# Four reorderings in a fused two-block transformer kernel on one core: first decay-scaled keys on ScalarE, VN additions ahead of the turns' low parts, gating scalings one step later, second norm block turned sooner

## The reference

```python
# block 1, delta rule: one step of the scan over chunks (both directions; the kernel uses chunks of 128)
v_new = u_i - einsum('bhcd,bhde->bhce', w_i, state)
o     = einsum('bhcd,bhde->bhce', q_i * exp(g_i), state) + einsum('bhcs,bhse->bhce', a_i, v_new)
k_dec = k_i * exp(g_last - g_i)
state = state * exp(g_last) + einsum('bhcd,bhce->bhde', k_dec, v_new)
# block 2
att = forgetting_attention(q, k, v, log_f)             # softmax((q k)/8 + c_i - c_j), causal
vg  = rmsnorm(vg, v_gain)                              # per group of 64: vg / sqrt(mean(vg^2)+eps) * gain
sg  = u * (tril(w_s) @ vg + b_s)
h   = h + concat([att, sg]) @ w_out
h   = h + conv_ffn(rmsnorm(h, norm_ffn_g), ...)        # the second norm block: "n2" in the kernel
```

## Time and profile before

| | us |
|---|---|
| median of three runs | 935.65 |
| the profiled execution's own time | 934.92 |
| its span, first to last instruction | 933.1 |
| TensorE busy | 909.5 |
| VectorE, ScalarE, GpSimd busy | 484.0, 455.1, 465.5 |

### The profile page before, as it was taken

One profiled execution on the slowest core, in us unless ns is written; L12 is line 12 of the kernel. 1 busy time (PEld: TensorE's weight loads), 2 busy tenths in 40 slices (PEclk: granted clock), 3 DMA queues, 4 the chain that ended last, 5 costly groups with the idle time before them and its releaser, 6 DMA issues.

```text
span 933.1 us, 11972 instructions
## 1 busy us (share of the span) xinstructions
PE 909.5 (97%) x4752; PEld 767.0 (82%) x4752; DVE 484.0 (52%) x814; ACT 455.1 (49%) x809; POOL 465.5 (50%) x264
## 2 busy tenths in 40 slices
PE   8999999999999999999998999999999999999997
PEld 6988778899998888788776888888888888888885
DVE  5779826898857443533654335333333334654434
ACT  7665597666545434447555336343333334423223
POOL 4454443986665433457786424444444444354440
PEclk9999999999999999999998999999999999999999
DMA  9522300000022714332321214223232222233202
GB/s 345 183 94 87 113 23 1 1 2 1 1 91 89 242 46 136 113 91 69 91 68 46 91 45 137 91 91 109 98 109 91 90 91 93 88 120 107 90 23 91
DMA packets 25303, 83.63 MB, mean 90 GB/s; under 512 B 3008, under 2 KB 3264, under 8 KB 25120
## 3 DMA queue, kind: packets, MB, share of 16 engines
q1 hardware_dynamic: 24240, 81.49, 26.5%
q10 hardware_dynamic: 1008, 1.38, 0.4%
HBM read 78.66 MB, written 2.10 MB: 87 GB/s over the span
## 4 chain that ended last, share of the span: by engine, by line
PE 81%; DVE 9%; POOL 5%; ACT 3%; issue 1%; DMA 1%; SPq 0%; POOLq 0%; DVEq 0%; ACTq 0%
PE bank L2165 78%; PE bank L2173 3%; DVE qk L1662 2%; DVE vc L1662 1%; POOL mb L1159 1%; DVE r L1656 1%; POOL mb L1163 1%; DMA xt<-in_xt 1%; POOL dd L1169 1%; ACT L1296 1%; POOL wl L1147 1%; DVE bank L1656 0%; ACT vc L1296 0%; POOL nh L1196 0%; ACT xh L1296 0%
## 5 line engine op out<-in xcount | busy, mean ns | idle before, releaser
L1147 POOL TENSOR_TENSOR wl<-raw,wh 128x1024 fp32r<-128x1024 f32 (+1 forms) x129 | 309.5, 2404 | 375.2 <-ACT wh L1296 375.1
L2165 PE MATMUL bank<-xh,wh 128*128 128x512 f32 (+1 forms) x536 | 206.9, 386 | 1.1 <-DVE xl L1656 1.1
L2165 PE MATMUL bank<-xl,wh 128*128 128x512 f32 (+1 forms) x536 | 205.2, 383 | 0.0
L2165 PE MATMUL bank<-xh,wl 128*128 128x512 f32 (+1 forms) x528 | 202.2, 383 | 0.0
L1296 ACT ACTIVATE wh<-raw 128x1024 fp32r<-128x1024 f32 (+2 forms) x132 | 136.0, 1035 | 124.6 <-PE bank L2165 119.1
L2165 PE MATMUL bank<-wh,xh 128*128 128x512 f32 (+1 forms) x352 | 141.6, 402 | 1.6 <-DVE xl L1662 1.0
L2165 PE MATMUL bank<-wh,xl 128*128 128x512 f32 (+1 forms) x352 | 135.1, 384 | 0.0
L2165 PE MATMUL bank<-wl,xh 128*128 128x512 f32 (+1 forms) x352 | 135.1, 384 | 0.0
L2165 PEld LDWEIGHTS bank<-xh,wh 128*128 128x128 f32 x536 | 100.8, 188 | 20.7 <-issue 1.5
L2165 PEld LDWEIGHTS bank<-xl,wh 128*128 128x128 f32 x536 | 100.8, 188 | 19.0
L2165 PEld LDWEIGHTS bank<-xh,wl 128*128 128x128 f32 x528 | 99.2, 188 | 19.7
(11 more groups left out here) (271 smaller groups left out, 1429.3 us busy)
## 6 DMA issues: line engine op xcount, KB each, us to landing
raw<-in_wflat SPq DMA_DIRECT2D x126, 512.0 KB, 3.4
xt<-in_xt SPq DMA_DIRECT2D x8, 256.0 KB, 4.0
h<-in_x SPq DMA_DIRECT2D x4, 512.0 KB, 7.2
h<-in_x SPq DMA_DIRECT2D x1, 2048.0 KB, 8.9
gain<-in_pr SPq DMA_DIRECT2D x3, 512.0 KB, 4.2
consts<-in_cf SPq DMA_DIRECT2D x1, 1088.0 KB, 9.5
raw<-in_wflat SPq DMA_DIRECT2D x4, 272.0 KB, 10.4
kh<-kh SPq DMA_DIRECT2D x8, 128.0 KB, 2.3
```

The costliest lines, as they stand in the source:

```text
L1147: e.tensor_tensor(WL[u % NS][:, 0:n], RAW[u % NS][:, 0:n], WH[u % NS][:, 0:n].bitcast(F32), ALU.subtract).then_inc(w_lo.up(u), 1)
L2165: return e.matmul(o, l, r_, start=start, stop=stop, skip_group_check=part)
```

## The change

Four edits of the list, one of which also moves work to another engine:

```diff
-    do("kd_first")
+    do("kd_first", 0)
     while step(gs):
         pass
+    do("kd_first", 1)
...
     w_ahead(30)
     scan_ks(3)
+    for d in range(2):
+        do("scan_out", d, 2)
     scan_qs(0, 3)
     scan_vn(0, 3)
...
     split("m1", 2, 1)
     split("m1", 3, 1)
-    for d in range(2):
-        do("scan_out", d, 2)
...
         for tb in range(4):
+            if i == 2 and tb == 3:
+                late(which, 1)
             do("last", u0, tb, src, ks)
...
-            if tb > 1:
-                split(which, tb - 2, 0)
-                split(which, tb - 2, 1)
+            if tb == 2 or tb == 3 and i == 1:
+                late(which, tb - 2)
...
-        if 8 <= n < 28 and n % 2 == 0 or n > 31:
+        if 8 <= n < 28 and n % 2 == 0 or n > 32:
             step(gg)
...
-        def kd_first():          # GpSimd
-            ...
-            for d in range(2):
-                cb = chunk(d, 0)
-                e.tensor_tensor(h3(SCAN[d]["KD"][:]), h3(KT[:, cb, :]), b4r(EGL[:, d, cb, :]), ALU.mult)...
+        def kd_first(d):         # ScalarE
+            cb = chunk(d, 0)
+            on.wait_ge(*gate_a.at("egl"))
+            on.wait_ge(*tok_a.at(("k", 3)))
+            on.wait_ge(*inv_v.at(("t", 0, 1)))
+            for h in range(4):
+                act(hs(SCAN[d]["KD"], h), hs(KT[:, cb, :], h), ACT.Copy, ..., scale=EGL[:, d, cb, h:h + 1])
```

More of the change, by code:

```diff
@@ L813, in program, with late @@
         G.let_go(("tok", U_OUT, tb))
+    def late(which, tb):
+        split(which, tb, 0)
+        split(which, tb, 1)
     def out_last(i, u0, src, which, ks):
@@ L835, in out_last @@
         do("scale", i, 3)
-    def late(which, tb):
-        split(which, tb, 0)
-        split(which, tb, 1)
     G.over(range(8))
@@ L1243, in scan_kd @@
             e.tensor_tensor(h3(SCAN[d]["KD"][:]), h3(KT[:, cb, :]), b4r(EGL[:, d, cb, :]), ALU.mult).then_inc(scan_g.up(("kd", d, r)), 1)
-        def kd_first():
-            on.wait_ge(*gate_a.at("egl"))
-            on.wait_ge(*tok_a.at(("k", 3)))
-            on.wait_ge(*inv_v.at(("t", 0, 1)))
-            for d in range(2):
-                cb = chunk(d, 0)
-                e.tensor_tensor(h3(SCAN[d]["KD"][:]), h3(KT[:, cb, :]), b4r(EGL[:, d, cb, :]), ALU.mult).then_inc(scan_g.up(("kd", d, 0)), 1)
         def fa_norm(n):
@@ L1287, in pool_engine @@
         return dict(finish=finish, prep=prep, prep_half=prep_half, inv_mb=inv_mb, inv_m=inv_m, inv_mt=inv_first, inv_d=inv_d, inv_tri=inv_tri, inv_x7=inv_x7, inv_causal=inv_causal, z_gain=z_gain, swa_o=swa_o,
-                    vb_first=vb_first, kd_first=kd_first, scan_vb=scan_vb, scan_kd=scan_kd, gm_w=gm_w, gm_sq=gm_sq, gm_gain=gm_gain, fa_norm=fa_norm, fa_low=fa_low)
+                    vb_first=vb_first, scan_vb=scan_vb, scan_kd=scan_kd, gm_w=gm_w, gm_sq=gm_sq, gm_gain=gm_gain, fa_norm=fa_norm, fa_low=fa_low)
     def scalar_engine(e):
@@ L1506, in swa_t @@
             act(PMT[n % 2][:, 0:nk], psum[SWA_T[n % 2]][:, 0:nk], ACT.Copy, swa_a.up(("pt", n)))
+        def kd_first(d):
[4 more added lines that the diff above has]
+            for h in range(4):
+                act(hs(SCAN[d]["KD"], h), hs(KT[:, cb, :], h), ACT.Copy, scan_a.up(("kd", d) if h == 3 else ("kd", d, h)),
+                    scale=EGL[:, d, cb, h:h + 1])
         def scan_vn(d, r):
@@ L1644, in scalar_engine @@
                     gate1=gate1, gate2=gate2, rope_sq=rope_sq, rope_root=rope_root, rope_keys=rope_keys, rope_t=rope_t, tok=tok, tok_end=tok_end, z_silu=z_silu, inv_decay=inv_decay, inv_mr=inv_mr,
-                    inv_x=inv_x, inv_d=inv_d, swa_e=swa_e, swa_t=swa_t, scan_v=scan_vn, scan_av=scan_av, scan_oq=scan_oq,
+                    inv_x=inv_x, inv_d=inv_d, swa_e=swa_e, swa_t=swa_t, kd_first=kd_first, scan_v=scan_vn, scan_av=scan_av, scan_oq=scan_oq,
                     dn_sq=dn_sq, forget=forget, cum_a=cum_a, gelu=gelu, qk2=qk2, fa_exp=fa_exp, fa_t=fa_t, fa_o=fa_o_, fa_split=fa_split,
@@ L2485, in scan_s @@
             p = bank(("s", d, r))
-            on.wait_ge(*scan_g.at(("kd", d, r)))
+            on.wait_ge(*(scan_g.at(("kd", d, r)) if r else scan_a.at(("kd", d))))
             on.wait_ge(*scan_a.at(("vn", d, r)))
```

## The result

The changed kernel takes 924.7 us (median of four executions, 923.39 to 926.8), the kernel before took 936.18 us in the same measurement (four, 935.13 to 936.98): a ratio of 0.9885 on record, interval 0.9861 to 0.991, so 1.15% faster (the two medians by themselves give 0.9877). 924.0 us was predicted. The profiled execution took 923.39 us in its own time, span 921.6, against the 923.3 that the prediction made for it.

The account below looks back on a forecast made before the run. TensorE's stream, busy 909.5 of 933.1 us, was taken as the bound. Gains 0.7 + 3.9 + 6.2 + 0.8 = 11.6 us took 934.92 to 923.3, plus 0.73 for the median: 924.0 us, range 922.9 to 928.2.

Parts of the forecast that it names:

- Part 1: Start of scan: first decay-scaled keys move from GpSimd to ScalarE, removing TensorE's wait for kd; gain 0.7 us.
- Part 2: Last scan step: additions of o go ahead of the low parts; gain 3.9 us, 2.2 wait plus 1.7 clock.
- Part 3: End of attention: gating norm one step later, so ptl comes earlier; gain 3.5 - 0.2 + 2.9 = 6.2 us.
- Part 4: Second norm: token block 1 turned ahead of the last 18 matmuls, removing a 1.07 us wait; gain 0.8 us.
- Busy time: Sign for the whole kernel: TensorE's busy time falls by some 4 us, its waits by at least 6.
- Table load: Gating norm's ScalarE load costs 1.28 us without drain; rival that it drains gives 926.6 us, chance 2%.
- the clock falls all the same: Rival: lowered clock stays behind one or both removed long waits; 925.7, 926.9 or 928.6 us, chance 15%.
- slower: Rival: denser work lowers the clock between 570 us and the end; 30 us of it gives 939 us, chance 3%.
- A new wait takes the removed one's place: Rival: ScalarE late at the gating norm, 925.3 us; a like gap at the scan's last step too, 926.6; chance 17%.
- clock terms: Full clock returns behind the removed waits for o and ptl, giving back 1.7 and 2.9 us.

Follow-up runs that it names:

- e8: Changed kernel with both first decay-scaled key multiplications (kd) put back on GpSimd; 923.92 us, one execution.
- e3: Changed kernel with the two additions to o moved back behind the low parts; 927.62 us, ratio 0.9918 to the kernel before.
- e1: Changed kernel with the gating norm's root and scalings again one step earlier; 929.6 us, ratio 0.9944 to the kernel before.
- e9: Changed kernel with token block 1 of the second norm turned behind the last 18 matmuls again; 927.91 us, one execution.
- e4: Changed kernel with the additions to o moved back and 8 unread matmuls in TensorE's wait for o; 926.76 us, ratio 0.991 to the kernel before.
- e2: Changed kernel with the gating norm one step earlier again and 13 unread matmuls in TensorE's wait for ptl; 929.17 us, ratio 0.9932.
- e11: e10 plus 13 unread matmuls in TensorE's wait for the last ptl; 925.99 us, ratio 0.9898 to the kernel before.
- e10: e7 with the gating norm's root and scalings again one step earlier; 927.81 us, ratio 0.9916 to the kernel before.
- e5: The changed kernel run again unaltered; 923.71 us, ratio 0.9896 to the kernel before.
- e6: Changed kernel with two inv_t turns moved into TensorE's wait for the last softmax tiles pm; 923.13 us, ratio 0.9898 to the kernel before.
- e7: e6 with the es additions and their exponentials replaced by 32 ScalarE activations of 128x1; 922.93 us, ratio 0.9887 to the kernel before.
- e12: Changed kernel with eight more 128x8 VectorE additions, four with an operand in PSUM, during GpSimd's four multiplications; 928.54 us, one execution.

## Why the prediction was right

The sum was 0.7 + 3.9 + 6.2 + 0.8 = 11.6; the marks give 0.87 + 4.01 + 6.09 + 0.89 = 11.86, and undoing one part at a time (e8, e3, e1, e9) gives 0.88, 4.08, 5.92 and 0.87.

- **Part 1**, 0.7 forecast, 0.87 measured. The gain is larger than the wait because of how a wait is counted: from the end of the matmul before it, 0.28 us behind that matmul's start. In the changed kernel `scan_s` starts 0.16 us behind the start of the matmul before it, ahead of that end. So without part 1 TensorE waits 0.75 (e8), and the marks differ by 0.88. The eight activations from SBUF took 2.44 us, not the 2.17 of those from PSUM, inside a gap that held them.
- **Part 2**, 3.9 forecast as 2.2 + 1.7, 4.01 measured, and e4 divides it into 2.4 and 1.65. The bank behind the last low part was hidden by 0.2 us in the forecast; by the timeline there is almost nothing left.
- **Part 3**, wait 3.5 forecast, 3.59 measured; clock less the new wait 2.7 forecast, 2.50 measured. The new wait at the third token block is some 0.05 us where 0.1 to 0.2 were forecast, so it is the clock's own term, 2.9, that was about 0.4 too large. This was the term at risk, since the clock was taken to follow the wait: e2, e4 and e11 show that at these places it does, and e10 shows that its size is not a constant.
- **Part 4**, 0.8 forecast, 0.89 measured. The new wait is 0.19 us and not the 0.4 to 0.5 forecast. Counted from the start of `pair` (553.48), block 3's `xs` ends after 4.04 us (4.2 forecast) and TensorE has finished half of the turns after 3.91 (3.8 forecast).
- **Busy time.** The forecast asked for a fall of some 4 us, the page shows 3.3; the six start-up matmuls on `zero` took 5.49 us instead of 4.53 in these two executions, so without them it is 4.3. TensorE's idle time (span less busy) fell from 23.6 to 15.4 us, by 8.2, of which 0.8 lie in the start-up; the forecast asked for at least 6.
- **Slips that changed nothing.** The prediction speaks of 24 matmuls and turns in another place; it is the eight turns of token block 1. And the terms named for the lower end of its range add up to 923.05 us, not 922.9.
- **Table load.** It begins at 497.34, and the `pth` ahead of it ends at 497.33; the root starts at 498.64, 1.30 us later. "ScalarE: Activation LUTs", section "What ACT_TABLE_LOAD costs", of the Trainium skill adds a drain of 1.38 us; in this load, as in the one of the earlier trace rows, none is seen, and the measurement decides.

Of the rivals, *the clock falls all the same* is refuted at both places (1.00 in the windows), and so is *slower*: with some 7.6 us of waits taken away, the long stretch still runs at 1.00. *A new wait takes the removed one's place* happened only as the 0.19 us. The mechanism was known for half of the gain only: that the clock belongs to the wait was argued from two neighbours in time, with the waits of 0.7 and 1.07 us as counter-examples; it is shown only by e2, e4 and e11.

That the sum was met to 0.1 us is in part luck. Its clock terms (1.7 + 2.9) were read from one execution in which the clock had fallen at both places, mean clock 0.993. On the chip of e5 the kernel before ran at a mean clock of 0.997 in five of nine executions and at 0.993 in one, and there the medians are 9.5 us apart (933.25 and 923.71), not 11.5.

## What to carry to other kernels

In a kernel whose TensorE is 97% busy, list its waits by length and price each with the clock that follows it: the two waits of 2.2 and 3.6 us cost 4.0 and 4.8 to 6.1 us in these profiles. Read the mean clock of several executions before counting on the clock's share. Where a wait can't be removed and the clock falls behind it, independent matmuls in it gain time even if their results are thrown away (1.8 us, e10 against e11). And where effects are smaller than the spread between executions, compare the times between fixed instructions of the bound engine's stream, not the totals.

## What had not been expected

**A 128x8 addition explains most of the spread.** In the stretch A-B the changed kernel has two faces. A good execution (the changed kernel's own profile) and a bad one (e1):

```profile
193.01 0.54 DVE L1659 TENSOR_TENSOR es<-rparams,mx 128x8 f32<-128x8 f32 x1
```

```profile
193.54 3.01 DVE L1659 TENSOR_TENSOR es<-rparams,mx 128x8 f32<-128x8 f32 x1
...
191.53 5.01 POOL L1188 TENSOR_TENSOR mp<-ds,consts 128x512 f32<-128x512 f32 x4
...
197.31 1.17 PE L2168 MATMUL bank<-xf,xf 128*128 128x192 f32 x8 [1.35 <-DVE xf L1659]
```

`es` ends with GpSimd's run of four multiplications (191.53 + 5.01 = 196.54 against 193.54 + 3.01 = 196.55), the `xf` queued behind it is late, and TensorE waits 1.35 us. It took 0.5 to 0.6 us in the profiles of before, the changed kernel, e4, e5, e6 and e8, and 3.0 in those of e1, e2, e3 and e9. With `es` off VectorE (e7, e10, e11) none of 14 executions strayed by more than 0.8 us from the others of its kernel, on two chips. On one of these e9 and e12 had the slow addition; on the other e6, which keeps `es` on VectorE, had two of five executions 1.6 to 1.9 us above its fastest. In the good execution it ended at 193.55, just behind the start of GpSimd's third multiplication (193.46); in the bad one it missed two such borders. The addition starts 2.04 us behind GpSimd's run in the one and 2.01 in the other, so what decides it is not to be seen in these rows.

**The same wait, with and without the clock.** In e2 and e3 the wait for `xf` (1.37 and 1.36 us) was followed by a clock of 1.00 and cost 1.75 us (A-B 48.25 and 48.23); in e1 and e9 (1.35 and 1.36 us) it was followed by half clock (0.50 from 198.5 to 201.5 in e1) and cost 3.15 (49.65). So at that length both happen. The spread of the changed kernel fits it (923.4 and 923.7 at a mean clock of 0.999, 925.7 at 0.998, 926.8 at 0.996), though only profiled executions show it.

The long waits are no different. The profile of the kernel before has about 10 us at half clock (0.50 in 298.5 to 301.8 and in 506.7 to 513.4; the longer wait ends at 507.61, so the clock fell while TensorE still stood) and a mean clock of 0.993. Of its 25 executions beside the later runs, nine have that mean and took 934.94 to 937.33 us; eight have 0.995 and six 0.997; and two have 0.999, which leaves room for less than 3 us at half clock in the whole execution (2 x 0.0015 x 932), and took 933.24 and 933.34. Only mean clock and span are on record of these two, but the kernel and its order of work are the same. So standing still is needed for the fall (e2, e4, e11) and doesn't always bring it. What decides it stays open.

**The gating multiplications** (`vg`, both operands in SBUF), one by one, before and then in the changed kernel:

```profile
504.22 1.46 DVE L1656 TENSOR_TENSOR vg<-vg,vss 128x512 f32<-128x512 f32 x1
505.61 1.75 DVE L1656 TENSOR_TENSOR vg<-vg,vss 128x512 f32<-128x512 f32 x1
```

```profile
499.74 1.81 DVE L1659 TENSOR_TENSOR vg<-vg,vss 128x512 f32<-128x512 f32 x1
501.48 0.68 DVE L1659 TENSOR_TENSOR vg<-vg,vss 128x512 f32<-128x512 f32 x1
```

Before, GpSimd was at work beside both (its `wl` until 505.14, its `xl` from 505.10 to 506.81). In the changed kernel its `xl` ran beside the first alone (499.71 to 501.01), and the second took 0.68 us, like the last two, with GpSimd at rest. A row that merges two instructions, as in the earlier trace rows and above, hides this. The forecast did not need it, since they had moved off the path; a plan that keeps such a pair on the path should price it by what GpSimd does beside it.
